# Turning and projecting the last tile but one in two parts in a hybrid GDN / window-attention layer on one Trainium2 core

## The chip, the core and the metric

One core of a Trainium2 chip runs the whole layer. Its engines each work through their own instruction list and meet at semaphores: TensorE (PE, matrix products and turns, that is transposes made by a product with the identity), VectorE (DVE), ScalarE (ACT), GpSimd (POOL) and SyncE (SP, which issues most transfers). The metric is the device time of one execution in microseconds (us).

## What is computed

1024 tokens of width 1024 pass through a mixing layer with two halves, and then through a mixture of experts. The change touches only the step that joins the halves and projects them.

```python
h = rms_norm(x, attn_norm_g)
proj = h @ w_in
...
y_a = rms_norm(gated_delta_rule(gq, gk, gv, log_a, beta)) * silu(a_z)      # 512 columns
y_b = swa_sink_attention(sq, sk, sv, swa_sinks)                            # 512 columns
x = x + jnp.concatenate([y_a, y_b], axis=-1) @ w_out
x = x + hier_moe(rms_norm(x, ffn_norm_g), ...)
```

`y_a` is the output of the gated delta rule, `y_b` that of the softmax attention over a window of 128 tokens.

## The kernel before

The tokens are worked in NT = 8 tiles of 128 (tile 0 to tile 7). `run_tiles` writes, for each engine, the same sequence: a start, `body(t, nx, pv, nn)` for t = 0 to 7, and `late(7)`. In a body, t is the tile whose delta rule and attention are worked, nx = t + 1 the tile whose input projection is worked ahead, and pv = t - 1 the tile whose output projection, norm and router are worked behind. In `body(7, None, 6, None)` no next tile is left, so TensorE has no input projection to fill with. After `late(7)` come the routing and 32 expert steps.

The order on an engine is the order in which the code is written; there is no scheduler. What matters here:

- On VectorE, body(t) ends with the results of tile t: first the attention columns of `y_mix` (L1379, semaphore `yb_ready`), then a chain of small steps and the delta rule's columns of `y_mix` (L1396, `ya_ready`), and after it the front work for the next tile (`gate_inputs`, `silu`, `gate_outputs`, `attention_norm`). The next body starts with L1250, which waits for `small_done`.
- On ScalarE, body(t) ends with `swa_squares`, `silu`, `gates` and `squares` of the next tile (L805, L810, L792 to L798, L814). `gates` starts when VectorE has done `gate_inputs` (`u_ready`), and `squares` when `qkvT` is there. The next body's copies of the turned `y_mix` (`copy_yT`, L835 and L836) are written behind them.
- On TensorE, body(t) begins with `turn_y(pv)`: it waits for both `ya_ready` and `yb_ready`, and turns all eight 128-column blocks of `y_mix` into PSUM banks pm[6] and pm[7]. ScalarE copies them to `yT` (the same memory as `pT`), which raises `yT_ready`. Behind `turn_y` stand the turns of `qkvT` (`kv_turned`), three small groups of products (they end with `small_done`), the products of k with k (`kk_done`) and, after VectorE's `diff_ready`, those of q with k (`qk_done`). Then come the six levels of the triangular inverse, which alternate between TensorE, ScalarE (copies of Y) and VectorE (updates of X and XT).
- `out_half(t, n, ks)` makes the output projection of 512 columns: one 128x512 product for each k in ks, with `yT[:, k, :]` and `wo_sb`. A tile needs 16 of them, k = 0 to 3 for the delta rule's columns and k = 4 to 7 for the attention's. The trace has two MATMUL records for each such product. In body(7) they are spread: five before the first turn of the inverse, three in level 0, four in level 1, four in level 2.
- `late(7)` already works in two parts: turn k = 4 to 7, eight products, turn k = 0 to 3, eight products.

The two calls in TensorE's body that the change replaces:

```python
                if pv is not None:
                    turn_y(pv)
...
                if nx is None:
                    pe.wait_ge(B.yT_ready, pv + 1)
                    pe.wait_ge(F.chunk_copied, 6 * NT)
                    out_half(pv, 0, range(0, 5))
```

Of the kernel before, what the change touches and what calls it, by code (L numbers as in the profile page):

```python
# [22 lines left out]
P = 128  # L23
# [42 lines left out]
def build(nc, x, attn_norm_g, w_in, conv_w, a_log, dt_bias, out_norm_g, q_norm_g, k_norm_g, sinks,  # L66
          w_out, ffn_norm_g, b_group, b_expert, w_router, w_gate_up, w_down, out, dbg=None):
    with ExitStack() as ctx:
# [114 lines left out]

        def late_banks(t):
            return (pm[0], pm[1]) if t == NT - 2 else (pm[6], pm[7])


        def flat(tile):
# [161 lines left out]
        def _(pe):  # L350
# [3 lines left out]
            def turn(o_, in_):  # L354
                return pe.transpose(o_, in_, ident[:, :])  # L355
# [50 lines left out]
            def out_half(t, n, ks=range(KD), first=0, last=KD - 1):  # L406
                for k in ks:
                    ins = mm(late_banks(t)[n][:, :], yT[:, k, :], wo_sb[:, k, n * 512:(n + 1) * 512], k == first, k == last)
                if ks[-1] == last:
                    ins.then_inc(B.out_done, 1)  # L410
# [28 lines left out]
                        pe.wait_ge(A.hots, c * AHEAD + t + 1)  # L439
                        mm(pm[0][:, 0:P], hot_mod[u], hot_row[u], u == 0, False)  # L440

            def late(t):
                pe.wait_ge(B.yb_ready, t + 1)
                for k in range(4, KD):
                    ins = turn(pm[7][:, (k % 4) * P:(k % 4 + 1) * P], y_mix[:, k * P:(k + 1) * P])
                ins.then_inc(B.y_turned, 1)
                pe.wait_ge(B.yT_ready, t + 1)
                for n in range(2):
                    out_half(t, n, range(4, KD), 4, 3)
                pe.wait_ge(B.ya_ready, t + 1)  # L450
                for k in range(4):
                    ins = turn(pm[2][:, k * P:(k + 1) * P], y_mix[:, k * P:(k + 1) * P])
                ins.then_inc(B.y_turned, 1)
                pe.wait_ge(B.yT_ready, t + 2)
                for n in range(2):
                    out_half(t, n, range(4), 4, 3)
                turn_xm(t)
                logits(t)
                rows_ahead()

            def body(t, nx, pv, nn):
# [7 lines left out]
                        project(nx, c, ks)  # L469

                ahead(1)
                if pv is not None:
                    turn_y(pv)

                pe.wait_ge(F.qkvT_ready, t + 1)
# [29 lines left out]
                    ins = mm(pm[5][:, h * P:(h + 1) * P], qkvT[:, H + h, :], qkvT[:, h, :])  # L505
                ins.then_inc(B.qk_done, 1)
                if nx is None:
                    pe.wait_ge(B.yT_ready, pv + 1)
                    pe.wait_ge(F.chunk_copied, 6 * NT)
                    out_half(pv, 0, range(0, 5))  # L510
                elif pv is not None:
                    out_half(pv, 1)
                ahead(2)
# [11 lines left out]
                for l in range(n):  # L525
                    if l:
                        pe.wait_ge(B.x_updated, 5 * t + l)
                    else:
                        pe.wait_ge(B.aT_ready, t + 1)
                    if l < n - 1:  # L530
                        pe.wait_ge(B.aTm_ready, 5 * t + l + 1)
                        for h in range(H):
                            for c in HALVES:
                                ins = mm(pm[3][c, h * CH:(h + 1) * CH], aTm[c, l % 2, h, 0:CH], Xd[c, h, :])
                    else:
                        for h in range(H):
                            ins = mm(pm[3][HI, h * CH:(h + 1) * CH], a10T[:, h, :], Xd[LO, h, :])
                    ins.then_inc(B.y_done, 1)
                    if l == 0:

                        if later(t):
                            pe.wait_ge(B.s_updated, t)
                        for h in range(H):
                            ins = mm(pm[4][:, h * P:(h + 1) * P], qkvT[:, H + h, :], S[:, h, :])
                        ins.then_inc(B.ks_done, 1)
                        if nx is None:
                            out_half(pv, 0, range(5, KD))
                        elif pv is not None:
                            logits(pv)
                    if nx is None:  # L550
                        if l == 1:
                            out_half(pv, 1, range(0, 4))
                        elif l == 2:
                            out_half(pv, 1, range(4, KD))
                        elif l == 3:
                            turn_xm(pv)
                        elif l == 4:
                            logits(pv)
                    if l == 1:
                        ahead(3, range(0, 4))  # L560
                    elif l == 2:

                        pe.wait_ge(F.qkn_ready, t + 1)
                        if later(t):
                            pe.wait_ge(B.lg_ready, t if nx is not None else t - 1)
                        for g in range(GRP):
                            turn(pm[6][:, g * P:(g + 1) * P],
                                 qkn[:, KVH * g:KVH * g + KVH, :].rearrange("p h d -> p (h d)"))
                        turn(pm[7][:, 0:P], qkn[:, QH:QH + KVH, :].rearrange("p h d -> p (h d)")).then_inc(B.swa_turned, 1)
                    elif l == 3:  # L570
                        ahead(3, range(4, KD))
                        ahead(4, range(0, 2))
                    elif l == 4:
                        ahead(4, range(2, KD))
                    elif l == 5:

                        pe.wait_ge(B.p_ready, t + 1)
                        for h in range(QH):
                            ins = turn(pm[6 + h // 4][:, (h % 4) * P:(h % 4 + 1) * P], scores(t)[:, h, :])
                        ins.then_inc(B.p_turned, 1)  # L580
                        ahead(5)
                    pe.wait_ge(B.y_copied, 6 * t + l + 1)
                    if l:
                        pe.wait_ge(B.xT_updated, 6 * t + l)
                    if l < n - 1:
                        for h in range(H):
                            for c in HALVES:
                                if l < n - 2 or c == LO:
                                    ins = mm(pm[2][c, h * CH:(h + 1) * CH], XTd[c, h, :], Yd[c, h, :])
                    else:  # L590

                        for h in range(H):
                            ins = mm(pm[2][:, h * P:(h + 1) * P], qkvT[:, h, :], S[:, h, :])
                    ins.then_inc(B.z_done, 1)
                    if l == 0:
                        pe.wait_ge(B.qkT_ready, t + 1)
                    for h in range(H):
                        if l < n - 1:
                            for c in HALVES:
                                ins = mm(pm[5][c, h * CH:(h + 1) * CH], Yd[c, h, :], XTd[c, h, :])  # L600
                        else:
                            ins = mm(pm[5][LO, h * CH:(h + 1) * CH], Yd[HI, h, :], XT[HI, h, CH:P])
                    ins.then_inc(B.zt_done, 1)
                    if l == 2:

                        pe.wait_ge(B.qT_ready, t + 1)
                        pe.wait_ge(B.kWin_ready, t + 1)
                        mm(pm[6][:, 0:P], ident[:, :], ident[:, :])
                        for g in range(GRP):
                            for kv, half in ((0, 0), (1, 1), (0, 1), (1, 0)):  # L610
                                keys = kWin[kv * DH:(kv + 1) * DH, 0:3:1 + half, :]
                                if half == 0:
                                    keys = kWin[kv * DH:(kv + 1) * DH, 0:2, :]
                                ins = mm(pm[6 + kv][half * CH:(half + 1) * CH, g * P:(g + 1) * P],
                                         qT[kv * DH:(kv + 1) * DH, g, half * CH:(half + 1) * CH], keys)
                        ins.then_inc(B.scores_done, 1)
# [143 lines left out]
        def _(act):  # L760
# [77 lines left out]
            def square_xm(t):  # L838

                act.wait_ge(B.xm_ready, 2 * t + 2)  # L840
                act.activation(y_mix[:, :], xr, ACT.Square, accum_out=bs[:, 88:89]).then_inc(B.ss2_ready, 1)

            def late(t):
                act.wait_ge(B.y_turned, t + 1)
                act.activation(yT[:, 4:8, :], heads(pm[7]), ACT.Copy).then_inc(B.yT_ready, 1)
                act.wait_ge(B.y_turned, t + 2)
                act.activation(yT[:, 0:4, :], heads(pm[2]), ACT.Copy).then_inc(B.yT_ready, 1)  # L847
                square_xm(t)
                act.wait_ge(B.late_step, VL * NT)
                act.activation(y_mix[:, :], xr, ACT.Copy, scale=bs[:, 89:90]).then_inc(B.hm_ready, 1)  # L850

            def body(t, nx, pv, nn):
# [3 lines left out]

                ahead(0)
                ahead(1)
                if pv is not None:
                    copy_yT(pv)  # L860
                act.wait_ge(B.kv_turned, t + 1)
                act.activation(vt[:, :, :], heads(pm[3]), ACT.Copy).then_inc(B.vt_ready, 1)
# [852 lines left out]
```

## Time and profile before

| what | value |
|---|---|
| median of 3 runs | 1025.11 us (1024.98 to 1025.66) |
| the profiled execution's own time | 1026.02 us |
| its span in the trace | 1024.2 us |
| TensorE busy | 959.2 us, 94% of the span |
| VectorE, ScalarE, GpSimd busy | 590.7, 208.8, 158.7 us |
| granted TensorE clock, mean | 0.973 |

A product record with "128*128 128x512" has a 128x128 operand that is held in the array and streams 512 columns. Columns of the timeline: start, duration, engine, line and operation, output and inputs, count, and the idle time ahead with what ended it. A granted clock of 1.00 is 2.4 GHz, 0.50 is 1.2 GHz. Starts are in us from the span's start. Body(6) ends on TensorE at 618.05 us, body(7) runs from 625.17 to about 682 us, and `late(7)` to 702 us.

### The profile page before, as it was taken

How to read it: one execution, taken by the hardware profiler on the slowest of the kernel's cores; microseconds unless marked ns; L12 is line 12 of the kernel's file. 1: busy time of each engine (PE TensorE's matmuls, PEld its weight loads, DVE VectorE, ACT ScalarE, POOL GpSimd, SP SyncE). 2: the span in 40 equal slices, each digit the busy share in tenths (PEclk: the TensorE clock that was granted, in tenths of full speed). 3: DMA queues.
4: the chain of work that ended last, by engine and by line, in shares of the span. 5: the costliest groups of instructions: out<-in, count | busy, mean ns of one | idle time of the engine just before them, and what ended most of it. 6: DMA issues, size and time to landing. Idle time of an engine off the chain costs nothing.

```text
span 1024.2 us, 19170 instructions
## 1 busy us (share of the span) xinstructions
PE 959.2 (94%) x7896; PEld 756.8 (74%) x7896; DVE 590.7 (58%) x1771; ACT 208.8 (20%) x494; POOL 158.7 (15%) x244
## 2 busy tenths in 40 slices
PE   5989999999999999999999996987899999999993
PEld 5687777687696697787878765565887887878872
DVE  2356875785775776675677468588324434444242
ACT  1233233331341332323323223110000000000000
POOL 7010010010010001001001003000323323334221
PEclk9999999999999999999999996997899999999997
DMA  9900101001000010010100119014457877879210
GB/s 318 351 21 2 43 1 43 22 22 42 21 23 21 22 42 22 22 43 1 43 22 1 42 32 359 15 49 165 123 193 278 304 249 262 298 267 326 89 59 28
DMA packets 48529, 109.71 MB, mean 107 GB/s; under 512 B 10288, under 2 KB 11568, under 8 KB 48432
## 3 DMA queue, kind: packets, MB, share of 16 engines
q1 hardware_dynamic: 32880, 82.87, 22.6%
q0 software_dynamic: 13824, 25.20, 7.2%
q8 instruction: 71, 1.16, 0.5%
q10 hardware_dynamic: 1728, 0.26, 0.1%
q14 instruction: 26, 0.21, 0.1%
HBM read 108.30 MB, written 25.17 MB: 130 GB/s over the span
## 4 chain that ended last, share of the span: by engine, by line
PE 88%; DVE 8%; issue 2%; ACT 1%; DMA 0%; DVEq 0%; ACTq 0%; POOL 0%; POOLq 0%
PE pm L352 83%; PE pm L355 5%; DVE X L1294 1%; DVE Y L1492 0%; DVE w_sb L986 0%; DVE X L1490 0%; DVE xt L1502 0%; DMA xt<-in_x 0%; DVE pqkv L1154 0%; DVE bs L1352 0%; DVE hT L1112 0%; DVE pqkv L1502 0%; DVE bs L977 0%; DVE bs L978 0%; DVE bs L976 0%
## 5 line engine op out<-in xcount | busy, mean ns | idle before, releaser
L352 PEld LDWEIGHTS pm<-hT,w_sb 128*128 128x128 f32 x1544 | 175.8, 193 | 6.3 <-DVE hT L1112 3.4
L352 PE MATMUL pm<-hT,w_sb 128*128 128x128 f32 x1544 | 176.9, 277 | 2.8 <-DVE hT L1112 2.8
L352 PE MATMUL pm<-w_sb,hT 128*128 128x512 f32 (+1 forms) x384 | 145.3, 529 | 0.0
L352 PE MATMUL pm<-wo_sb,pT 128*128 128x512 f32 x256 | 114.6, 599 | 1.4 <-ACT pT L847 0.7
L352 PEld LDWEIGHTS pm<-w_sb,hT 128*128 128x128 f32 x384 | 70.6, 190 | 56.2 <-issue 51.2
L1154 DVE SCALAR_TENSOR_TENSOR pqkv<-ci,cw,pqkv 128x128 f32<-128x128 f32 x288 | 77.7, 347 | 19.0 <-ACT pqkv L786 18.6
L352 PE MATMUL pm<-ctmp,w_sb 128*128 128x128 f32 x768 | 88.4, 276 | 0.1
L352 PEld LDWEIGHTS pm<-wo_sb,pT 128*128 128x128 f32 x256 | 47.6, 192 | 55.1 <-issue 53.2
L352 PEld LDWEIGHTS pm<-ctmp,w_sb 128*128 128x128 f32 x768 | 86.8, 192 | 0.3 <-issue 0.3
L1584 POOL TENSOR_TENSOR tail<-tail,rows 128x512 f32<-128x512 f32 x8 | 10.2, 1270 | 465.1 <-ACT aTm L805 465.1
L352 PE MATMUL pm<-w_sb,Y 128*128 128x512 f32 x152 | 68.7, 595 | 4.1 <-DVE Y L1492 4.1
L947 ACT ACTIVATE X<-pm 128x256 f32<-128x256 f32 x32 | 12.3, 383 | 285.4 <-PE pm L352 256.2
L352 PE MATMUL pm<-ci,w_sb 128*128 128x128 f32 x448 | 51.2, 275 | 0.0
L352 PEld LDWEIGHTS pm<-w_sb,Y 128*128 128x128 f32 x152 | 27.4, 190 | 31.6 <-issue 31.6
L352 PEld LDWEIGHTS pm<-ci,w_sb 128*128 128x128 f32 x448 | 50.6, 192 | 0.0
L1294 DVE TENSOR_TENSOR X<-X,pm 128x256 f32<-128x256 f32 (+1 forms) x40 | 16.8, 419 | 49.0 <-PE pm L352 48.3
L1502 DVE SCALAR_TENSOR_TENSOR xt<-pm,w_sb,xt 128x512 f32<-128x512 f32 x16 | 11.6, 749 | 50.6 <-PE pm L352 50.6
L879 ACT ACTIVATE Y<-pm 128x256 f32<-128x256 f32 (+1 forms) x48 | 18.4, 383 | 104.6 <-PE pm L352 104.6
L1200 DVE TENSOR_TENSOR sc<-sc,pm 128x512 f32<-128x512 f32 x16 | 11.0, 688 | 49.0 <-PE pm L352 49.0
L1502 DVE SCALAR_TENSOR_TENSOR pqkv<-pm,w_sb,pqkv 128x512 f32<-128x512 f32 x16 | 11.6, 749 | 44.2 <-PE pm L352 44.2
L352 PEld LDWEIGHTS pm<-Y,aTm 64*64 64x64 f32 x576 | 21.7, 134 | 19.3 <-issue 17.8
L1502 DVE SCALAR_TENSOR_TENSOR tail<-pm,w_sb,tail 128x512 f32<-128x512 f32 x16 | 12.0, 751 | 38.4 <-PE pm L352 38.4
(288 smaller groups left out, 1489.4 us busy)
## 6 DMA issues: line engine op xcount, KB each, us to landing
w_sb<-in_w_gate_up SPq DMA_DIRECT2D x12, 2048.0 KB
w_sb<-in_w_down SPq DMA_DIRECT2D x12, 1024.0 KB
w_sb<-in_w_in SPq DMA_DIRECT2D x5, 2048.0 KB, 17.2
wo_sb<-in_w_gate_up SPq DMA_DIRECT2D x4, 2048.0 KB
xt<-in_x SPq DMA_DIRECT2D x8, 512.0 KB, 3.5
wo_sb<-in_w_out SPq DMA_DIRECT2D x1, 4096.0 KB, 22.2
sc<-in_x SPq DMA_DIRECT2D x8, 512.0 KB, 3.4
out<-sc SPq DMA_DIRECT2D x8, 512.0 KB, 2.8
```

The lines of the kernel that those rows point to most:

```text
L352: return pe.matmul(o_, lhsT=l_, rhs=r_, start=start, stop=stop, skip_group_check=True)
L355: return pe.transpose(o_, in_, ident[:, :])
L879: act.activation(Yd[rows_], heads(pm[3], CH)[rows_], ACT.Copy).then_inc(B.y_copied, 1)
L947: act.activation(tnh, pm[2 + p % 2][:, 0:DE], ACT.Tanh, scale=0.5).then_inc(M.tanh_ready, 1)
L1154: ins = v.scalar_tensor_tensor(cv[:, i, :], ci[:, i, j:j + P], cw[:, j, i:i + 1], cv[:, i, :], ALU.mult, ALU.add)
L1200: v.tensor_tensor(xr[:, 512 * n:512 * n + 512], xr[:, 512 * n:512 * n + 512], late_banks(self.t)[n][:, :], ALU.add).then_inc(B.xm_ready, 1)
L1294: v.tensor_tensor(Xd[rows_], Xd[rows_], heads(pm[2], CH)[rows_], ALU.subtract).then_inc(B.x_updated, 1)
L1502: ins = v.scalar_tensor_tensor(y[:, n * 512:n * 512 + 512], pm[4 + 2 * b + n][:, :], gate, y[:, n * 512:n * 512 + 512], ALU.mult, ALU.add)
L1584: g.tensor_tensor(qk_in[:, 0:QH, :], qk_in[:, 0:QH, :], gqk[:, None, 0:DH].broadcast_to([P, QH, DH]), ALU.mult)
```

## The change

Tile 6 (t = NT - 2) is turned and projected in two parts in body(7), as tile 7 is in `late(7)`. The new function `window_rows` is the first part of the old `late`, and body(7) calls it where `turn_y` stood. It turns k = 4 to 7 into pm[7] as soon as `yb_ready` is there, waits for ScalarE's copy, makes the eight products with k = 4 to 7 (both halves of the output), waits for `ya_ready` and turns k = 0 to 3. The eight products with k = 0 to 3 stay in the body: two ahead of the first turn of the inverse, two in each of levels 0, 1 and 2. ScalarE's `copy_halves` makes the two copies with a wait before each; it stands where `copy_yT` stood. `halves_turned` counts the semaphores, `ya_bank` names the bank.

```diff
+            def window_rows(t):
                 pe.wait_ge(B.yb_ready, t + 1)
                 for k in range(4, KD):
                     ins = turn(pm[7][:, (k % 4) * P:(k % 4 + 1) * P], y_mix[:, k * P:(k + 1) * P])
                 ins.then_inc(B.y_turned, 1)
-                pe.wait_ge(B.yT_ready, t + 1)
+                pe.wait_ge(B.yT_ready, halves_turned(t, 0))
+                if t == NT - 2:
+                    pe.wait_ge(F.chunk_copied, 6 * NT)
                 for n in range(2):
                     out_half(t, n, range(4, KD), 4, 3)
                 pe.wait_ge(B.ya_ready, t + 1)
                 for k in range(4):
-                    ins = turn(pm[2][:, k * P:(k + 1) * P], y_mix[:, k * P:(k + 1) * P])
+                    ins = turn(ya_bank(t)[:, k * P:(k + 1) * P], y_mix[:, k * P:(k + 1) * P])
                 ins.then_inc(B.y_turned, 1)
...
-                if pv is not None:
+                if nx is None:
+                    window_rows(pv)
+                elif pv is not None:
                     turn_y(pv)
...
                 if nx is None:
-                    pe.wait_ge(B.yT_ready, pv + 1)
-                    pe.wait_ge(F.chunk_copied, 6 * NT)
-                    out_half(pv, 0, range(0, 5))
+                    pe.wait_ge(B.yT_ready, halves_turned(pv, 1))
+                    out_half(pv, 0, range(0, 2), 4, 3)
...
-                            out_half(pv, 0, range(5, KD))
+                            out_half(pv, 0, range(2, 4), 4, 3)
...
-                            out_half(pv, 1, range(0, 4))
+                            out_half(pv, 1, range(0, 2), 4, 3)
                         elif l == 2:
-                            out_half(pv, 1, range(4, KD))
+                            out_half(pv, 1, range(2, 4), 4, 3)
```

TensorE at the start of body(7), before:

```order
L352 MATMUL pm4<-V_S,XT_qkT 128x128 x4
L355 MATMUL pm6<-ident,y_mix 128x128 [waits yb_ready,ya_ready]
L355 MATMUL pm6<-ident,y_mix 128x128 x3
L355 MATMUL pm7<-ident,y_mix 128x128 x4
L355 MATMUL pm2<-ident,qkvT 128x128 [waits o_ready,v_ready,s_updated,xT_updated,qkvT_ready]
L355 MATMUL pm2<-ident,qkvT 128x128 x3
L355 MATMUL pm3<-ident,qkvT 128x128 x4
L352 MATMUL pm5<-upper,fs 128x128 [waits la_ready]
```

The same place in the changed kernel:

```order
L359 MATMUL pm4<-V_S,XT_qkT 128x128 x4
L362 MATMUL pm7<-ident,y_mix 128x128 [waits yb_ready]
L362 MATMUL pm7<-ident,y_mix 128x128 x3
L359 MATMUL pm0<-wo_sb,pT 128x512 [waits chunk_copied,yT_ready]
L359 MATMUL pm0<-wo_sb,pT 128x512 x3
L359 MATMUL pm1<-wo_sb,pT 128x512 x4
L362 MATMUL pm6<-ident,y_mix 128x128 [waits ya_ready]
L362 MATMUL pm6<-ident,y_mix 128x128 x3
L362 MATMUL pm2<-ident,qkvT 128x128 [waits o_ready,v_ready,s_updated,xT_updated,qkvT_ready]
L362 MATMUL pm2<-ident,qkvT 128x128 x3
```

The eight products with `wo_sb`, and a wait for `yT_ready`, now stand ahead of the turns of `qkvT`.

ScalarE around the end of body(6) and the start of body(7), in the changed kernel (in the kernel before the two copies into `pT` stand at the same place, from pm6 and pm7, and only the first of them waits):

```order
L806 ACTIVATE fs<-fs 128x4 [waits u_ready]
L808 ACT_TABLE_LOAD
L808 ACTIVATE fs<-fs 128x4 [waits exp_ready]
L809 ACT_TABLE_LOAD
L809 ACTIVATE fs<-tail 128x4
L812 ACTIVATE gsz<-tail 128x512 [waits ya_ready]
L828 ACTIVATE ctmp<-qkvT 128x512 [waits qkvT_ready]
L859 ACTIVATE pT<-pm7 128x512 [waits y_turned]
L861 ACTIVATE pT<-pm6 128x512 [waits y_turned]
L881 ACTIVATE kd_vt<-pm3 128x512 [waits kv_turned]
```

The copies have not moved: they stand behind the gates and squares of tile 7 as before. Nothing moves on VectorE, GpSimd and SyncE.

## Rows read from the trace of the kernel before

**Rows 1.** The page, chain of work that ended last: shares of the span.

```profile
PE 88%; DVE 8%; issue 2%; ACT 1%; DMA 0%; DVEq 0%; ACTq 0%; POOL 0%; POOLq 0%
```

**Rows 2.** That chain in order of time, 608 to 639 us: start, us, what.

```profile
617.16 0.76 DVE y_mix L1379 x2
...
624.42 0.69 DVE y_mix L1396
...
636.99 0.44 DVE ctmp L1255
```

**Rows 3.** Timeline of TensorE, end of body(6) and body(7) to level 2.

```profile
616.99 1.06 PE L352 MATMUL pm<-V_S,XT_qkT 128*128 128x128 f32 x8
625.17 1.97 PE L355 MATMUL pm<-ident,y_mix 128*128 128x128 f32 x8 [7.12 <-DVE y_mix L1396]
...
630.88 2.08 PE L352 MATMUL pm<-upper,fs 128*128 128x128 f32 x8 [1.59 <-DVE fs L1130]
...
633.46 1.84 PE L352 MATMUL pm<-ones,ctmp 128*128 128x1 f32 x8
...
637.47 2.07 PE L352 MATMUL pm<-qkvT 128*128 128x128 f32 x8 [0.25 <-DVE ctmp L1255]
639.34 5.29 PE L352 MATMUL pm<-wo_sb,pT 128*128 128x512 f32 x10
644.62 0.68 PE L352 MATMUL pm<-eye,aTm 64*64 64x64 f32 x16
...
647.39 2.74 PE L352 MATMUL pm<-wo_sb,pT 128*128 128x512 f32 x6
...
651.88 3.70 PE L352 MATMUL pm<-wo_sb,pT 128*128 128x512 f32 x8
...
657.33 3.70 PE L352 MATMUL pm<-wo_sb,pT 128*128 128x512 f32 x8
```

**Rows 4.** Timeline of ScalarE, same stretch.

```profile
625.62 0.21 ACT L792 ACTIVATE fs<-fs 128x4 f32<-128x4 f32 x1 [9.93 <-DVE fs L1120]
...
629.29 0.61 ACT L814 ACTIVATE ctmp<-qkvT 128x512 f32<-128x512 f32 x1
629.81 0.57 ACT L835 ACTIVATE pT<-pm 128x512 f32<-128x512 f32 x1
```

**Rows 5.** Timeline of VectorE, same stretch and the side work of levels 1 and 2.

```profile
635.86 0.15 DVE L1250 COPY bs<-pm 128x4 f32<-128x4 f32 x1
...
644.14 0.42 DVE L1277 TENSOR_TENSOR aTm<-eye,aTm 128x256 f32<-128x256 f32 x1
...
652.52 1.14 DVE L1334 SCALAR_TENSOR_TENSOR kd_vt<-kd_vt,bs,V_S 128x128 f32<-128x128 f32 x4
...
659.43 0.32 DVE L1004 TENSOR_REDUCE w_sb<-w_sb 128x24 f32<-128x96 f32 x1
```

**Rows 6.** Timeline of TensorE in late(7): the same eight products of tile 7.

```profile
683.17 7.13 PE L352 MATMUL pm<-wo_sb,pT 128*128 128x512 f32 x16 [0.69 <-ACT pT L845]
```

**Rows 7.** Timeline of TensorE at the start of body(6), at full clock.

```profile
550.75 1.04 PE L355 MATMUL pm<-ident,qkvT 128*128 128x128 f32 x8
...
552.88 1.03 PE L352 MATMUL pm<-ones,ctmp 128*128 128x1 f32 x8
```

**Rows 8.** Stretches: length, busy us of PE, PEld, DVE, ACT, POOL, then granted clock.

```profile
618.05:625.17 7.12, 0.00 (x0) 0.00 (x1) 6.53 (x20) 0.00 (x0) 0.00 (x0) 0.67 1.04 400
...
630.88:639.34 8.46, 8.21 (x37) 7.92 (x37) 7.60 (x32) 2.24 (x11) 5.33 (x31) 0.50 0.87 329
639.34:644.62 5.28, 5.28 (x11) 2.00 (x11) 4.96 (x15) 0.00 (x0) 0.00 (x0) 0.84 0.00 0
...
709.40:712.80 3.40, 0.00 (x0) 0.00 (x0) 3.12 (x16) 0.00 (x0) 0.00 (x0) 0.50 1.05 409
```

**Rows 9.** TensorE in the routing: a resumption after 3.27 us of idleness.

```profile
718.21 3.78 PE L352 MATMUL pm<-xt,ci 128*128 128x128 f32 x16 [3.27 <-DVE xt L1063]
```

**Rows 10.** The clock there, by the us.

```profile
722.00:723.00 1.00, 1.00 (x6) 1.00 (x6) 0.15 (x1) 0.00 (x0) 0.00 (x0) 0.54 0.77 262
```

More of the change, by code:

```diff
@@ L185, in late_banks, with ya_bank, halves_turned @@
             return (pm[0], pm[1]) if t == NT - 2 else (pm[6], pm[7])
+        def ya_bank(t):
+            return pm[6] if t == NT - 2 else pm[2]
+        def halves_turned(t, n):
+            return NT - 2 + 2 * (t - NT + 2) + n + 1
         def flat(tile):
@@ L440, in rows_ahead @@
                         mm(pm[0][:, 0:P], hot_mod[u], hot_row[u], u == 0, False)
-            def late(t):
+            def window_rows(t):
                 pe.wait_ge(B.yb_ready, t + 1)
@@ L451, in late @@
                 for k in range(4):
-                    ins = turn(pm[2][:, k * P:(k + 1) * P], y_mix[:, k * P:(k + 1) * P])
+                    ins = turn(ya_bank(t)[:, k * P:(k + 1) * P], y_mix[:, k * P:(k + 1) * P])
                 ins.then_inc(B.y_turned, 1)
-                pe.wait_ge(B.yT_ready, t + 2)
+            def late(t):
+                window_rows(t)
+                pe.wait_ge(B.yT_ready, halves_turned(t, 1))
                 for n in range(2):
@@ L841, in square_xm, with copy_halves @@
                 act.activation(y_mix[:, :], xr, ACT.Square, accum_out=bs[:, 88:89]).then_inc(B.ss2_ready, 1)
+            def copy_halves(t):
+                act.wait_ge(B.y_turned, halves_turned(t, 0))
+                act.activation(yT[:, 4:8, :], heads(pm[7]), ACT.Copy).then_inc(B.yT_ready, 1)
+                act.wait_ge(B.y_turned, halves_turned(t, 1))
+                act.activation(yT[:, 0:4, :], heads(ya_bank(t)), ACT.Copy).then_inc(B.yT_ready, 1)
             def late(t):
[L844 to L847, printed above, removed]
+                copy_halves(t)
                 square_xm(t)
@@ L858, in body @@
                 ahead(1)
-                if pv is not None:
+                if nx is None:
+                    copy_halves(pv)
+                elif pv is not None:
                     copy_yT(pv)
```

## The prediction

> **What bounds the kernel now.** I read the shares of the chain that ended last, then that chain in order of time, then the timelines of the engines around its one long stretch off TensorE. The chain is on TensorE for 88% of the span and on VectorE for 8% [rows 1]. Between body(6) and body(7) it leaves TensorE: attention columns (L1379) at 617.16, delta rule columns (L1396) at 624.42, L1255 at 636.99 [rows 2]. TensorE ends body(6) at 618.05 and idles 7.12 us until both parts of `y_mix` are there [rows 3]. The granted clock falls in that gap (mean 0.67), is 0.50 for the next 14 us, and comes back inside the stretch 639.34 to 644.62 [rows 8]. From L1250 at 635.86 to L1277, which ends at 644.56, VectorE has one unbroken chain [rows 5]; the first turn of the inverse, at 644.62, waits for its end [rows 3]. Before L1250 VectorE is itself the late one: `small_done` comes at 633.46 + 1.84 = 635.30 [rows 3], 0.56 us earlier. Behind the turn, levels 0 to 2 are TensorE's: the projection's products sit between the groups of the inverse and end last in each level [rows 3].
>
> **Part 1: the early turn.** The four turns of the attention columns can start at 618.05. They cost some 0.6 us in an idle gap: nothing.
>
> **Part 2: the wait for the copy, on which the result hangs.** TensorE then waits for ScalarE's copy into `yT`. In ScalarE's list that copy stands behind the gates and squares of tile 7 [the ScalarE piece above]. Those cannot run early: the first of them, L792, waits 9.93 us for VectorE's L1120, which comes after the delta rule columns, and starts at 625.62 [rows 4]. The squares L814 start at 629.29 and the copy L835 right behind them at 629.81, though the turns it reads had ended at 625.17 + 1.97 = 627.14 [rows 3, 4]. So today's copy is already held by its place, not by its input. Turning earlier leaves the new first copy at 629.81, ending at 630.38, and TensorE goes on at 630.4. The eight products do not fill the gap at 618: they start behind it, and the gap grows to about 11.8 us.
>
> The Trainium skill bears on this in "TensorE: Matmul & The Clock Gate", "Architectural detail: the array is 16× 32×32, not 1× 128×128": it says that ScalarE and VectorE are strict first in, first out, while TensorE can pull weight loads ahead of matmuls. By that rule the copy cannot pass the gates; were the queue free, the result would be the gain of rival 3. The rows of ScalarE agree with the rule.
>
> **Part 3: what now stands behind it.** Behind the wait and the eight products are queued the turns of k = 0 to 3, the turns of `qkvT`, the three small groups, and so `small_done`, L1250 and everything of tile 7.
> - Eight products at full clock take 7.1 us [rows 6]. They now start at half clock. How long it stays there is the unknown. Where the same kind of products resumed at 639.34, the mean of 0.84 over 5.28 us means (1.00 - 0.84) / 0.50 x 5.28 = 1.7 us of half clock [rows 8]; in the routing, products from 718.21 on waited until 722.9 (a mean of 0.54 in the us from 722), 4.7 us [rows 9, 10]. Each us at half clock costs half a us. I take the middle, 3.2 us, so 7.1 + 1.6 = 8.7 us. The ends are 7.9 and 9.5 us.
> - Four turns, half of 1.04 us: 0.5 us. Turns of `qkvT` to the end of `small_done`, at full clock as in body(6): 552.88 + 1.03 - 550.75 = 3.2 us [rows 7].
> - `small_done` then comes at 630.4 + 8.7 + 0.5 + 3.2 = 642.8. VectorE's L1250 started at 635.86 [rows 5], so tile 7's chain is **6.9 us later** (6.1 to 7.7). VectorE had nothing else to do in that time, so nothing of it comes back there.
>
> **Part 4: what the moved products give back.** One product costs 3.70 / 4 = 0.925 us at full clock, and level 0's three cost 2.74 [rows 3].
> - Ahead of the first turn: five become two. Today they end at 644.62, just when L1277 ends at 644.56, so the three removed give under 0.1 us; VectorE's chain from 637.43 (end of L1255) to 644.56 is 7.1 us whatever TensorE does [rows 2, 3, 5].
> - Level 0: three become two, 0.9 us. Level 1: four become two, 1.85. Level 2: four become two, 1.85. These are on the chain, as long as VectorE's side work fits the shorter levels. Measured within today's levels it does: in level 1 it ends at 652.52 + 1.14 = 653.66, and with two products fewer the next group would start at 651.88 + 1.85 = 653.7; in level 2 it ends at 659.75, and two products and five turns would end at 659.8 at the earliest (657.33 + 1.85, and some 0.6 us for the turns) [rows 3, 5]. Together **4.6 us back**. The bound from above is 16 - 8 = 8 products, 7.4 us, if the first three counted too.
>
> **Part 5: a second gap.** After q with k (about 1.05 us at full clock, as for other groups of eight) and two products (1.85), TensorE now idles 7.1 - 2.9 = 4.2 us for L1277; today 0. In a gap of 3.4 us in the routing the clock was at half [rows 8]. So I expect a fall ahead of level 0. Its price is between 0 (no fall, or back before level 0) and about 3.5 us (all of the first turn, X, k with S and two products at half clock: their 0.7 + 0.7 + 1.1 + 1.85 us at most nearly twice over). Level 0 and 1 hold wide products, which brought the clock back soon at 639.34, so I take **1.5 us**.
>
> The page has a rule that speaks against the change here ("HAM oscillation — how this bites in real kernels"): gaps of TensorE that are long enough put the clock back to half, and the work behind each gap runs slow. By the rule both gaps cost; without the second cost the sum below would be 1.5 us less.
>
> **Sum.** 6.9 - 4.6 + 1.5 = +3.8 us. Everything later (late(7), the routing, the 32 expert steps) hangs on tile 7's chain and moves with it; the expert weights' loads had ended by 638 us and do not come nearer. The span of 1024.2 us becomes 1028.0, the profiled run's 1026.02 becomes 1029.8. The median of the runs is 0.9 us under the profiled run, so I forecast 1025.1 + 3.8 = **1028.9 us**. With the ends of parts 3 and 5 its own range is 6.1 - 4.6 + 0 = +1.5 to 7.7 - 4.6 + 3.5 = +6.6: 1026.6 to 1031.7.
>
> **Rivals.**
> 1. *The clock hardly costs anything*: it returns in the first of the eight products and does not fall again. Then 6.1 - 4.6 = +1.5 or, with no half clock at all in the eight products, 7.1 + 0.5 + 3.2 + 630.4 - 635.9 - 4.6 = +0.7: 1025.8 to 1026.6, within 0.2%. For it: wide products brought it back in 1.7 us. Against it: a gap of 11.8 us, and a second one.
> 2. *The clock stays down*: from 630.88 to 639.34 TensorE was busy for 8.21 of 8.46 us and stayed at half [rows 8]. Were all eight products slow, 14.2 - 8.7 = 5.5 us more, and the second gap at its full price, 2.0 more: +11, 1036. Against it: that stretch held narrow products, while those of 639.34 are wide.
> 3. *Faster: the products do fill the gap.* The place is ScalarE's copy of pm[7]. If it ran at 618.7, before the gates, the products would run 619.4 to 626.5 at a clock still high, the turns to 628, still ahead of `la_ready` at 630.8; `small_done` would be no later than 635.3, and the 4.6 us of part 4 would be a pure gain: 1020.5 us. It decides for faster from the point where that copy ends before about 626 us (626 + 7.1 + 3.7 = 636.8, less than 4.6 behind today). ScalarE is indeed idle from 615.7 to 625.6 [rows 4]. Against it: the copy is written behind the gates, and nothing in the trace shows ScalarE passing a waiting instruction.
> 4. *It does not do what it says*: this is the forecast itself, in so far as the products wait for the gates.
>
> **How the numbers follow.** Forecast (+1.5 to +6.6): 0.72. Rival 1 and near it: 0.15. Rival 2: 0.07. Rival 3: 0.06. About 0.2% (2 us) is what a measurement of this kernel can tell from no change; the forecast's lowest part, under +2, falls within it and weighs 0.03. So faster 0.06, same 0.17, slower 0.77. The range goes from 1026.0, inside rival 1, to 1033.0, a little into rival 2; outside lie rival 3, part of rival 1 and most of rival 2, under 0.2.
>
> **What would show it.** In the profile of the changed kernel: TensorE's four turns at about 618.1; then idleness until about 630.4, ended by ScalarE's copy, whose start stays at 629.8; eight products of 8 to 9.5 us, the first at half clock; L1250 at about 642.8, with VectorE idle some 7 us before it; a gap of 4 us ahead of the first turn of the inverse; products of level 2 that start 3.6 us behind those of level 1 instead of 657.33 - 651.88 = 5.45 us. I am wrong if the copy runs near 619, if L1250 starts before 640, or if the levels do not shorten by some 4.6 us in all.

## The result and the profile after

| | kernel before | changed kernel |
|---|---|---|
| median | 1025.05 us (1024.73 to 1025.66, 4 runs) | 1032.28 us (1031.37 to 1033.12, 4 runs) |
| span of the profiled execution | 1024.2 us | 1031.3 us |
| mean granted clock | 0.973 | 0.974 |

The ratio is 1.0074 with a 95% interval of 1.006 to 1.0087: the change costs 7.2 us, 6.1 to 8.9 by the interval. I had forecast 3.8. The sign and the place were right; the size was half.

The timeline of TensorE in the changed kernel from the end of body(6) to level 2, against [rows 3] (start, duration, engine, line, operation, inputs, count, and the idle time ahead):

```profile
618.20 1.06 PE L359 MATMUL pm<-V_S,XT_qkT 128*128 128x128 f32 x8
619.19 0.66 PE L362 MATMUL pm<-ident,y_mix 128*128 128x128 f32 x4
631.65 9.65 PE L359 MATMUL pm<-wo_sb,pT 128*128 128x512 f32 x16 [11.80 <-ACT pT L859]
641.14 0.60 PE L362 MATMUL pm<-ident,y_mix 128*128 128x128 f32 x4
...
643.71 1.03 PE L359 MATMUL pm<-ones,ctmp 128*128 128x1 f32 x8
...
653.53 0.92 PE L359 MATMUL pm<-eye,aTm 64*64 64x64 f32 x16 [4.27 <-DVE aTm L1296]
654.93 1.12 PE L359 MATMUL pm<-X,aTm 64*64 64x64 f32 x16 [0.48 <-ACT X L894]
655.98 2.07 PE L359 MATMUL pm<-V_S,qkvT 128*128 128x128 f32 x8
657.85 3.27 PE L359 MATMUL pm<-wo_sb,pT 128*128 128x512 f32 x4
...
662.87 1.98 PE L359 MATMUL pm<-wo_sb,pT 128*128 128x512 f32 x4
...
666.60 1.98 PE L359 MATMUL pm<-wo_sb,pT 128*128 128x512 f32 x4
```

ScalarE and VectorE in the same stretch, against [rows 4, 5]:

```profile
630.50 0.61 ACT L828 ACTIVATE ctmp<-qkvT 128x512 f32<-128x512 f32 x1
631.02 0.58 ACT L859 ACTIVATE pT<-pm 128x512 f32<-128x512 f32 x1
```

```profile
644.78 0.16 DVE L1269 COPY bs<-pm 128x4 f32<-128x4 f32 x1 [7.62 <-PE pm L359]
```

And stretches of the changed kernel, against [rows 8] (length, busy us of PE, PEld, DVE, ACT, POOL, then the granted clock): the wait, the eight products, the second gap, from the first turn to level 1, levels 1 and 2.

```profile
619.70:631.65 11.95, 0.15 (x3) 0.01 (x1) 9.40 (x26) 4.70 (x8) 0.98 (x1) 0.64 1.04 400
631.65:641.14 9.49, 9.49 (x17) 4.04 (x18) 5.07 (x18) 0.00 (x0) 5.54 (x32) 0.73 0.77 292
649.26:653.53 4.27, 0.00 (x1) 0.00 (x0) 4.08 (x10) 0.00 (x0) 0.00 (x0) 1.00 0.00 0
653.53:662.26 8.73, 8.19 (x77) 5.56 (x77) 1.79 (x5) 0.77 (x2) 0.00 (x0) 0.61 0.00 0
662.26:669.86 7.60, 7.54 (x103) 4.86 (x105) 5.62 (x20) 1.46 (x4) 0.00 (x0) 1.00 0.01 2
```

The four early turns ran at 619.19 and bought nothing: the copy still starts right behind the squares (L828, then L859), TensorE idles 11.80 us for it, and eight products stand between it and everything of tile 7. Both gaps go with half clock: it is granted from about 623.1 on, inside the first, and from about 653.8 on, 0.3 us behind the end of the second (0.55 and 0.91 are the means of the us from 623 and from 653).

Two updates of X on VectorE, ahead of levels 2 and 3, with the room that its side work leaves:

```profile
665.51 0.42 DVE L1313 TENSOR_TENSOR X<-X,pm 128x256 f32<-128x256 f32 x1 [0.87 <-PE pm L359]
...
669.86 0.42 DVE L1313 TENSOR_TENSOR X<-X,pm 128x256 f32<-128x256 f32 x1 [0.84 <-PE pm L359]
```

The end of body(6), the same work in both kernels, starts 1.21 us later in this execution (618.20 against 616.99). That offset is already there after the first projection, long before any changed line: its piece of the chain lasts 41.88 us here and 40.67 us before.

```profile
12.89 41.88 PE pm L359 x240
```

In the us from 18 to 19 the trace has seven products there, in the kernel before twelve: the slow pace of the start lasted some 3 us longer. The clock column shows 1.00 in these us in both executions, so that the clock is the reason is not shown. It is a difference between executions, and it is taken off below:

| place | before | changed | later by, less 1.21 |
|---|---|---|---|
| VectorE's first step of body(7) | 635.86 | 644.78 | 7.7 |
| first turn of the inverse | 644.62 | 653.53 | 7.7 |
| start of level 1's products with X | 651.27 | 662.26 | 9.8 |
| last update of X in level 2 | 662.30 | 669.86 | 6.35 |
| first turns of late(7) | 681.82 | 690.22 | 7.2 |
| 64 products of the first expert step | 728.14 | 737.33 | 8.0 |

The span ends 7.1 us later, not 8.0 + 1.2: in the profiled execution before, the clock fell once more near the end, under the last wide expert products (the first line is from before, the second from the changed kernel), 1.7 us, and 0.4 us go in the first 64 expert products (7.69 us before, 7.31 here). No run ties that to the change.

```profile
1004.83 5.37 PE L352 MATMUL pm<-wo_sb,Y 128*128 128x512 f32 x8 [2.01 <-DVE Y L1492]
1013.62 3.67 PE L359 MATMUL pm<-wo_sb,Y 128*128 128x512 f32 x8 [2.01 <-DVE Y L1511]
```

### The profile page after: what moved, and what is told of

Its sections match the earlier page's. It is cut to its first block, busy times and chain, and to the rows that moved or that the text cites. A ratio compares the mean times of both kernels' runs of the same rounds, so it can differ in the third digit from the quotient of the medians.

```text
span 1031.3 us, 19169 instructions
## 1 busy us (share of the span) xinstructions
PE 958.2 (93%) x7896; PEld 755.8 (73%) x7896; DVE 590.3 (57%) x1771; ACT 209.2 (20%) x494; POOL 158.9 (15%) x244
## 3 DMA queue, kind: packets, MB, share of 16 engines
q8 instruction: 71, 1.16, 0.5%
## 4 chain that ended last, share of the span: by engine, by line
PE 88%; DVE 8%; issue 2%; ACT 1%; DMA 0%; DVEq 0%; ACTq 0%; POOL 0%; POOLq 0%
PE pm L359 83%; PE pm L362 5%; DVE X L1313 1%; DVE Y L1511 0%; DVE w_sb L1005 0%; DVE X L1509 0%; DVE xt L1521 0%; DMA xt<-in_x 0%; DVE pqkv L1173 0%; DVE bs L1371 0%; DVE hT L1131 0%; DVE bs L995 0%; DVE bs L997 0%; DVE bs L996 0%; DVE pqkv L1521 0%
## 5 line engine op out<-in xcount | busy, mean ns | idle before, releaser
L359 PE MATMUL pm<-wo_sb,pT 128*128 128x512 f32 x256 | 117.9, 613 | 13.2 <-ACT pT L859 12.5
L1603 POOL TENSOR_TENSOR tail<-tail,rows 128x512 f32<-128x512 f32 x8 | 10.2, 1274 | 466.1 <-ACT aTm L819 466.1
## 6 DMA issues: line engine op xcount, KB each, us to landing
w_sb<-in_w_down SPq DMA_DIRECT2D x12, 1024.0 KB, 5.5
```

Source lines behind the costliest of these rows:

```text
L359: return pe.matmul(o_, lhsT=l_, rhs=r_, start=start, stop=stop, skip_group_check=True)
L1603: g.tensor_tensor(qk_in[:, 0:QH, :], qk_in[:, 0:QH, :], gqk[:, None, 0:DH].broadcast_to([P, QH, DH]), ALU.mult)
```

## The experiments

Theory A: the cost is the place of ScalarE's copy. It holds up the eight products, and these hold up tile 7; the two gaps of TensorE cost half clock on top. The rivals were that splitting costs in itself (B, C), that the levels cannot get shorter (D), and that the wait alone is the cost (E). All times below are medians, with the ratio to the kernel before on the same chip. The changed kernel was not run again beside them, so a difference against it compares medians of different series; the kernel before had 1024.66 to 1025.05 us in these series.

For the main places of the table above, this is how much later (us) each profiled execution is than the kernel before, less its own offset at the end of body(6):

| place | changed | e1 | e2 | e7 | e5 | e8 | e9 | e6 |
|---|---|---|---|---|---|---|---|---|
| VectorE's first step | 7.7 | 0.0 | 7.0 | 5.2 | 0.0 | 0.5 | 7.0 | 0.0 |
| first turn of the inverse | 7.7 | 0.0 | 7.0 | 5.2 | 3.1 | 4.7 | 7.0 | 0.7 |
| level 1's products with X | 9.8 | 0.6 | 6.2 | 4.3 | 2.2 | 3.8 | 4.4 | -1.9 |
| level 3's products with X | 6.35 | -2.8 | 2.7 | 0.9 | -1.2 | 0.4 | -0.7 | -7.0 |
| first turns of late(7) | 7.2 | -2.8 | 2.7 | 0.9 | 0.2 | 0.4 | -0.7 | -7.0 |
| first expert step | 8.0 | -2.6 | 3.0 | 0.8 | 0.8 | 0.7 | -0.4 | -7.0 |

### Only the copy moved: e1_copy_early

```diff
                     silu(nx)
+                    if nx == NT - 1:
+                        copy_window(t)      # the copy of pm[7] into yT, tile 6
                     gates(nx)
```

`copy_window` is the first half of `copy_halves`, which leaves it out for tile 6.

> The changed kernel with one edit: ScalarE's copy of the turned window rows of tile 6 stands ahead of the gates of tile 7 instead of behind its squares. Theory A (the place of the copy costs the time, the clock adds to it): the copy starts at about 619 us in place of 631, the eight products run some 619.9 to 627, and VectorE's first step of body(7) is not later than in the kernel before (about 636). The levels give 4.6 us back, and the idle 4.3 us ahead of the first turn of the inverse still puts level 0 at half clock, some 3.2 us. So 1025.1 - 4.6 + 3.2 = 1023.7 us, within 1020.5 and 1025. Theory B (the split itself costs: the turns in two parts, the waits, or levels that do not get shorter): 1027 us or more, and the first step of body(7) later than 638 us.

1023.96 us, ratio 0.9995 (0.9983 to 1.0006): 8.3 us faster than the changed kernel, and not told apart from the kernel before. TensorE and ScalarE there:

```profile
619.06 0.66 PE L362 MATMUL pm<-ident,y_mix 128*128 128x128 f32 x4
620.40 7.13 PE L359 MATMUL pm<-wo_sb,pT 128*128 128x512 f32 x16 [0.69 <-ACT pT L859]
...
645.70 0.68 PE L359 MATMUL pm<-eye,aTm 64*64 64x64 f32 x16 [1.99 <-DVE aTm L1302]
```

```profile
619.75 0.60 ACT L859 ACTIVATE pT<-pm 128x512 f32<-128x512 f32 x1 [2.97 <-PE pm L362]
626.71 0.21 ACT L806 ACTIVATE fs<-fs 128x4 f32<-128x4 f32 x1 [6.36 <-DVE fs L1145]
```

The products run where they were meant to, at full clock. Body(6) ended 1.08 us later than before in this execution, and 645.70 - 1.08 = 644.62, the very time of before: the delay of 7.7 us is gone. Nothing else changed in this kernel, so the place of the copy made it. The ScalarE row also shows that the copy disturbs nothing: L806 waits for VectorE for another 6.36 us. The clock is still at half from 633 to 643, and again in level 0:

```profile
633.00:643.60 10.60, 9.43 (x34) 6.97 (x32) 9.50 (x41) 0.73 (x2) 4.45 (x29) 0.52 0.58 220
645.70:650.90 5.20, 4.71 (x43) 3.98 (x44) 1.31 (x3) 0.77 (x2) 0.00 (x0) 0.67 0.00 0
```

In level 0 that costs 1.5 us (from the first turn to level 1 are 652.95 - 645.70 = 7.25 us, in e2 below 5.79), so that by level 3 this execution is 2.8 us ahead of the kernel before and not 4.3. The median is only 1.0 us ahead of it. The profiled execution, 1022.46 us, is one of the fastest of the eleven (1022.21 to 1026.70); where the others lose the rest these traces do not show. Theory B falls.

### The gaps filled: e2, e3, e4 and e7

```diff
+            def fill(bank, n):
+                for _i in range(n):
+                    mm(bank[:, :], wo_sb[:, 0, 0:P], wo_sb[:, 0, 0:512])
...
                 ins.then_inc(B.y_turned, 1)
+                if t == NT - 2:
+                    fill(pm[6], 11)         # first gap: e3 and e4; 13 in e7
                 pe.wait_ge(B.yT_ready, halves_turned(t, 0))
...
                     out_half(pv, 0, range(0, 2), 4, 3)
...
+                if nx is None:
+                    fill(pm[7], 4)          # second gap: e2, e4, e7
```

> The changed kernel with four products of 128x512 into the unused bank pm[7], whose result nobody reads, between the two projection products and the first turn of the inverse, where TensorE idles 4.27 us. Theory A: the clock does not fall ahead of level 0, which runs at full clock; level 0 becomes 3.2 us shorter and nothing else changes there: 1032.3 - 3.2 = 1029.1 us. Theory B (levels 0 to 2 give less than 4.6 us for another reason than the clock, say ScalarE's copies or VectorE's side work): no change, 1032.3 us.

1028.65 us, ratio 1.004 (1.0027 to 1.0054): 3.6 us less than the changed kernel. Its level 0:

```profile
651.23 0.68 PE L359 MATMUL pm<-eye,aTm 64*64 64x64 f32 x16 [0.84 <-DVE aTm L1302]
...
653.01 1.16 PE L359 MATMUL pm<-V_S,qkvT 128*128 128x128 f32 x8
654.00 1.88 PE L359 MATMUL pm<-wo_sb,pT 128*128 128x512 f32 x4
...
657.02 0.68 PE L359 MATMUL pm<-X,aTm 64*64 64x64 f32 x16
```

From the first turn to level 1's products are 657.02 - 651.23 = 5.79 us here, 8.73 in the changed kernel and 651.27 - 644.62 = 6.65 before. So one product less gives 0.86 us, as counted, and half clock behind the second gap costs 2.94 us. The products with S take 1.16 us here and 2.07 in the changed kernel. The median fell by more than these 2.9 us: in this execution the clock was back earlier in the eight products as well, which no edit touches (VectorE's first step is 7.0 us late and not 7.7).

> The changed kernel with eleven products of 128x512 into the unused bank pm[6], whose result nobody reads, ahead of the wait for ScalarE's copy, where TensorE idles 11.8 us. Theory A: the products end about when the copy does, the eight projection products behind them run at full clock in 7.0 us instead of 9.5, and all of tile 7 is 2.5 us earlier: 1032.3 - 2.5 = 1029.8 us. Level 0 stays at half clock. Theory B (the clock costs nothing here, since VectorE or ScalarE is late anyway): 1032.3 us.

1032.03 us, ratio 1.0073 (1.0059 to 1.0086): a miss. The filling was too short. Eleven products took 9.61 us, where 0.925 us each would have made 10.2, and the clock fell 1 us into the eight products:

```profile
619.02 9.61 PE L359 MATMUL pm<-wo_sb 128*128 128x512 f32 x22
630.99 8.83 PE L359 MATMUL pm<-wo_sb,pT 128*128 128x512 f32 x16 [2.37 <-ACT pT L865]
```

```profile
619.02:628.63 9.61, 9.60 (x24) 3.99 (x22) 8.47 (x25) 2.40 (x4) 0.00 (x0) 1.00 1.04 400
631.00:632.00 1.00, 1.00 (x3) 0.51 (x4) 1.00 (x3) 0.00 (x0) 0.92 (x3) 0.96 1.04 383
632.00:633.00 1.00, 1.00 (x3) 0.48 (x2) 0.97 (x3) 0.00 (x0) 0.92 (x3) 0.50 1.06 389
```

The clock fell here behind an idle stretch of only 2.37 us, and the products gained 0.8 us instead of 2.5. The median moved by 0.3 us, which by itself would fit theory B as well; e7 decides between them.

> Both fillings. Theory A: the two savings add up, 1032.3 - 2.5 - 3.2 = 1026.6 us; what is left over the kernel before, about 1.5 us or less, is the cost of the order alone (a delay of about 5.1 us against 4.6 us given back). Theory B: 1032.3 us. A third outcome, 1029 or so, would say that the two gaps are not independent.

1027.52 us, ratio 1.0027 (1.0017 to 1.0037). That is e2 and the small gain of the short filling, 0.9 us above what was expected, by the same miss.

> As e4_fill_both, with thirteen filling products in the first gap in place of eleven, so that they reach up to the copy (about 0.4 us short of it). Theory A: now the eight projection products run at full clock, 7.0 us in place of 8.7, which e4 did not reach since TensorE idled 2.4 us behind its filling. 1027.5 - 1.7 = 1025.8 us. What is then left, within 1 us of the kernel before, is the price of the order alone. Theory B: as e4, 1027.5 us.

1025.91 us, ratio 1.0014 (1.0003 to 1.0024), as expected. Now the eight products are at full clock (the last line is their stretch, with the granted clock):

```profile
619.01 11.32 PE L359 MATMUL pm<-wo_sb 128*128 128x512 f32 x26
630.99 7.13 PE L359 MATMUL pm<-wo_sb,pT 128*128 128x512 f32 x16 [0.65 <-ACT pT L867]
```

```profile
630.99:637.96 6.97, 6.97 (x17) 3.10 (x17) 5.07 (x18) 0.00 (x0) 5.31 (x30) 1.00 1.03 387
```

This kernel has the order of the changed one and neither of the two half clocks. It is 6.4 us faster than the changed kernel and about 1 us slower than the one before. By its rows that is 7.7 - (9.49 - 6.97) = 5.2 us of delay, against 4.3 us that come back from there to level 3: 0.9 us. The changed kernel is 6.35 us late at the same place. So half clock behind the two gaps costs 5.4 us there (2.5 and 2.9), and the order itself 0.9. The changed kernel loses 1.65 us more between level 3 and the experts, and this one does not; it lies behind the two gaps and their half clock, and where it comes from stays open.

### What of the delay is the wait, and what the products: e5 and e8

```diff
                 ins.then_inc(B.y_turned, 1)
-                pe.wait_ge(B.yT_ready, halves_turned(t, 0))      # kept here too in e8
...
-                for n in range(2):
-                    out_half(t, n, range(4, KD), 4, 3)
                 pe.wait_ge(B.ya_ready, t + 1)
...
                 ins.then_inc(B.qk_done, 1)
+                pe.wait_ge(B.yT_ready, halves_turned(pv, 0))
...
+                for n in range(2):
+                    out_half(pv, n, range(4, KD), 4, 3)
                 out_half(pv, 0, range(0, 2), 4, 3)
```

> The changed kernel with TensorE's eight window products moved behind the products of q with k, so that no wait for the first copy stands ahead of the turns of qkvT. Theory A (the cost is what is queued behind the wait): VectorE's first step of body(7) is back at about 636 us, 8 us earlier than in the changed kernel. Ten products then stand behind q with k (639.3) and end at about 649 us, some 4.5 us behind VectorE, which takes back the 4.6 us of the levels: about 1025 us, within 1023.5 and 1027. Theory C (turning the two parts apart, or ScalarE's two separate waits, costs in itself): 1029 us or more, with the first step of body(7) later than 639 us.

1025.76 us, ratio 1.0003 (0.9994 to 1.0012), as expected. VectorE starts body(7) at 636.83, with an offset of 0.97 us at the end of body(6): 635.86, as before. The ten products then are the late ones: the first turn starts at 648.67 - 0.97 = 647.70, 3.1 us later than before, where I had expected 4.5:

```profile
639.99 8.75 PE L359 MATMUL pm<-wo_sb,pT 128*128 128x512 f32 x20
648.67 0.68 PE L359 MATMUL pm<-eye,aTm 64*64 64x64 f32 x16
```

The split turns and ScalarE's two waits are all in this kernel, and its time is not told apart from that of the kernel before. Theory C falls.

> As e5_products_behind, but TensorE again waits for ScalarE's first copy ahead of the turns of the delta rule's columns; the eight products stay behind q with k. It prices the wait without the products. Theory A: the wait ends at about 631.6, the turns and the three small groups behind it are narrow and run at half clock (1.0 + 2.0 + 4.6 us), so VectorE's first step comes at about 639, some 2.2 us later than in e5: 1025.8 + 2.2 = 1028.0 us. Theory E (the wait alone is the cost, the products only follow it): nearly the changed kernel's 1032 us.

1025.64 us, ratio 1.0007 (0.9995 to 1.0018): a miss, since it is not told apart from e5, where I had expected 2.2 us more. VectorE and the clock there:

```profile
636.67 0.16 DVE L1275 COPY bs<-pm 128x4 f32<-128x4 f32 x1 [0.39 <-PE pm L359]
```

```profile
630.77:635.50 4.73, 4.73 (x24) 4.73 (x24) 4.29 (x17) 2.23 (x10) 3.92 (x16) 0.51 1.06 391
635.50:638.28 2.78, 2.13 (x19) 1.94 (x18) 2.33 (x9) 0.02 (x1) 1.85 (x17) 1.00 0.88 343
```

Body(6) ended 0.34 us late in it, so VectorE's first step is 636.67 - 0.34 - 635.86 = 0.5 us late. I had put all narrow work behind the gap at half clock, by the 8.46 us of it in [rows 8]; here the clock was back at 635.5, after 4.7 us. At VectorE's first step the wait alone costs 0.5 us of the 7.7, the eight products behind it 7.2. Theory E falls. The wait is cheap for three reasons in the rows: in the kernel before TensorE stands until 630.88 for VectorE's front work anyway [rows 3], so that the small groups start only 2.2 us later here (633.04 less the offset); the early return of the clock makes up 1.2 us of it; and VectorE has 0.56 us to spare. Without that return it would have been some 1.6 us, an estimate from these rows. What the wait lets through first is dear.

That the whole time equals e5's is in part chance. In e8 the clock was at half again from about 638.8 to 642.2, and the ten products took 10.00 us (8.75 in e5), so its first turn is 1.6 us later than e5's, and so is its level 3. The execution of e5 lost 1.4 us between level 3 and late(7), and that of e8 none. So up to level 3 the wait cost 1.6 us in these two executions.

### The version that wins: e6, and its halves

The spread, in e6 together with the early copy of e1, in e9 without it:

```diff
-                    out_half(pv, 0, range(0, 2), 4, 3)      # ahead of the first turn
+                    out_half(pv, 0, range(0, 4), 4, 3)
+                    out_half(pv, 1, range(0, 2), 4, 3)
...
-                            out_half(pv, 0, range(2, 4), 4, 3)      # level 0
...
-                            out_half(pv, 1, range(0, 2), 4, 3)      # level 1
+                            out_half(pv, 1, range(2, 3), 4, 3)
...
-                            out_half(pv, 1, range(2, 4), 4, 3)      # level 2
+                            out_half(pv, 1, range(3, 4), 4, 3)
```

> The early copy of e1_copy_early, and the eight products of the delta rule's columns spread anew: six ahead of the first turn of the inverse, where TensorE waits for VectorE, none in level 0, one in level 1, one in level 2. Theory A: level 0 loses 2.7 us against the kernel before, levels 1 and 2 some 2.8 each, 8.3 us in all; the six products end 1 to 2 us behind VectorE since they start at half clock; no half clock in level 0. So 1025.1 - 8.3 + 1.5 = 1018.3 us, within 1016.5 and 1021. Theory D (with so few products ScalarE's copies and VectorE's side work bound the levels): no better than e1_copy_early less its half clock, 1020.5 us or more.

1018.44 us (1017.15 to 1019.28, 6 runs), ratio 0.9934 (0.9921 to 0.9946): 6.4 us faster than the kernel before by the medians, and 13.8 us faster than the changed one.

```profile
641.81 6.04 PE L359 MATMUL pm<-wo_sb,pT 128*128 128x512 f32 x12
647.78 0.68 PE L359 MATMUL pm<-eye,aTm 64*64 64x64 f32 x16
...
651.85 0.68 PE L359 MATMUL pm<-X,aTm 64*64 64x64 f32 x16
...
654.72 0.68 PE L359 MATMUL pm<-X,aTm 64*64 64x64 f32 x16
```

Six real products fill the time in which TensorE waits for VectorE; they end 0.7 us behind it (647.78, less an offset of 2.47 us, is 645.31 against 644.62). From the first turn to level 1 are 4.07 us at a granted clock of 1.00 (6.65 before), and level 1 takes 2.87 us (5.45 before). The clock in level 0:

```profile
647.78:651.85 4.07, 3.53 (x73) 3.07 (x72) 1.12 (x3) 0.77 (x2) 0.00 (x0) 1.00 0.00 0
```

> The changed kernel with the spread of e6_early_spread (six products ahead of the first turn, none in level 0, one each in levels 1 and 2), and without the early copy. Theory A: the first step of body(7) stays 7.7 us late, but the 4.3 us gap ahead of the first turn is filled with four projection products, so level 0 runs at full clock (3.2 us) and the levels lose four products more (3.7 us): 1032.3 - 6.9 = 1025.4 us, the level of the kernel before. Against e6 it is then 7 us slower, which is the price of the copy's place in the queue. Theory D (the gain of e6 came from the early copy alone): 1029 us or more.

1026.27 us, ratio 1.0005 (0.9995 to 1.0015): the new spread alone takes 6.0 us off the changed kernel. Its six products and the first turn:

```profile
648.57 5.32 PE L359 MATMUL pm<-wo_sb,pT 128*128 128x512 f32 x12
654.72 0.68 PE L359 MATMUL pm<-eye,aTm 64*64 64x64 f32 x16 [0.84 <-DVE aTm L1295]
```

Only the early copy lies between it and e6. It is worth 7.8 us by the medians (taken on two chips; 7.3 us by the ratios) and 6.3 us by the rows at level 3, where the delay of VectorE's first step is 7.0 us in this execution. That is the price of the copy's place once more, from the other side. Theory D falls as well: e9 gains without the early copy, and e6 is below the 1020.5 us that theory D set as its floor.

## Why the prediction was right or wrong

- **The place of the copy** (parts 1 and 2). Right, and now shown by e1 and by e9 against e6. The gap of 11.8 us, the copy directly behind the squares and the restart 0.05 us behind its end (631.02 + 0.58 to 631.65) came as worked out; less the offset, the copy starts at 629.81, the time of before. Rival 3 was the same mechanism with the copy early; e1 built it. It did not give 1020.5 but 1024.0. Rival 3 had left out the half clock behind the second gap, which is in part 5 and cost 1.5 us here, and the levels gave 0.3 us less; the rest of the 3.5 us stays open.
- **Eight products, 8.7 us** (part 3). They took 9.49 us. The mean clock of 0.73 means (1.00 - 0.73) / 0.50 x 9.49 = 5.1 us at half. This is one of the two terms that were sized too low: 3.2 us of half clock taken, 5.1 measured. My ends, 1.7 and 4.7 us, were the two returns I had looked up, and this case lay outside both. The lower one was also misread: at 639.34 no work resumed. TensorE had been busy since 630.88, so from there to the return at 641 are 10.1 us, and 1.7 us is only the last piece of them. Nor does the width of the products separate the two cases, as rival 2 has it: in the routing the clock came back under products of 128 columns [rows 9, 10]. The delay of VectorE's first step was 7.7 us instead of 6.9, the upper end of what I had given.
- **What the levels give back** (part 4). 4.6 us forecast; 0.86 in level 0 (e2 against before), 1.7 in level 1 and 1.7 in level 2: 4.3 us. The side work of VectorE fits, with 0.87 and 0.84 us to spare ahead of its updates. The three products taken out ahead of the first turn gave nothing, as said: TensorE idles 4.27 us there.
- **The second gap** (part 5). This is the term that failed most: 1.5 us forecast, 2.9 us measured by e2. I had the bound (3.5) right and took a value near its middle, on the argument that wide products bring the clock back soon. That argument rests on the same misread 1.7 us. The gap of 3.4 us in the routing was a weak example too, since the clock was at half there before the gap began (0.64 is the mean of the us from 709). In this kernel it came back only at 660.6, 7 us after the first turn.
- **Everything later moves with it.** Not quite. Between level 2 and the experts the changed kernel loses 1.65 us more (6.35 to 8.0 in the table), 0.85 of it up to late(7). There the clock is at half from about 677.7 to 684.5, nearly 7 us, where before it was so from 671.7 to 675.1. My sum had no term for it, and no experiment isolates it. The length of that stretch does not explain it alone: in e7 the clock is at half from about 672.8 to 679.6, as long, and nothing is lost between level 3 and late(7). Nor does the second gap decide it: e3, which leaves it open, loses the same 1.65 us (5.5 at level 3, 7.2 at the experts), while e1, which leaves it open too, loses 0.3. The cause stays open. The sentence on the expert weights holds for six of the loads only; one more pair goes into `wo_sb`, which is free only behind late(7), and is issued at 704.5 in the kernel before. Its first product runs at 786.4, so it bears on nothing here.
- **Size.** 3.8 us forecast: 0.8 more in part 3, 0.3 less given back, 1.4 more in part 5, 1.65 more behind it, and 1.2 - 2.1 us at the two ends of the profiled executions, which is chance: 7.1. The median of the runs differs by 7.2 us, the same size.

The page of the Trainium skill quoted in part 2 says that ScalarE is strictly first in, first out: the copy waited 11.2 us with its input ready (619.8 to 631.02) while ScalarE stood idle until 626.84 for the entry ahead of it, so this trace agrees. The rule of its section on oscillation, that long gaps of TensorE put the work behind them at half clock, agrees too: e7 fills both gaps, the eight products and level 0 then run at full clock, and 6.4 us go. Long gaps are not the only case in these traces, as the last section shows.

## What to carry to other kernels

Work moved ahead of a waiting engine only gains if every link of its chain moves: here the products moved on TensorE, but the copy between turn and product stayed in ScalarE's list behind work that waits for VectorE, and the products then held up the critical tile. Before such a move, walk the chain across the engines and write down, for each link, what stands ahead of it in its own list and when that ends. And count a new gap of TensorE twice, once as a wait and once for the clock of what comes behind it; where real work is left to place, it belongs into that gap.

## What the runs showed of the hardware

- In the kernel before the clock fell at about 671.7, with no idle stretch of TensorE above 0.79 us in the 7 us ahead of it. A gap of 2.37 us of TensorE, behind 9.6 us of full work, was followed by a fall of the granted clock from 1.00 to 0.50 (e3, at 632). In e1 TensorE idled 2.47 us ahead of 631.96 and was at 1.00 in the us from 632, but at 0.51 in the next, under narrow products. Short gaps are no safeguard.
- From the end of the last idle stretch of over 1 us to full clock took 10.1 us (before, 630.88 to 641.0), 4.7 us (before, from 718.21), 4.7 us (e8) and 5.1 us (the changed kernel). Products of 128 columns and fewer left it at half for 8.46 us in one execution and not beyond 4.7 us in another. The length of one return is no bound for the next.
- The executions of one unchanged piece, the first projection, lasted 40.5 to 42.0 us in the eleven profiles (before, changed, e1 to e9), 1.5 us that no edit touches. For effects of 1 us, spans of single profiles have to be set against a common point.
